# Issuing the up matrices of three of four experts from ScalarE's queue

## The chip, the cores and the metric

The kernel runs on one core of one Trainium2 chip. The metric is the device time of one execution in microseconds; of several runs the median is given. A "unit" below is one half of an expert's weight matrix, a transfer of 2048 KB (128 partitions of 4096 float32 numbers).

## What is computed

One inference step of one decoder layer: a combined projection, differential attention and a short convolution, an output projection, and a mixture of experts. The change touches the last of these alone. For 264 tokens (256 prompt rows and 8 sample rows) it is

```
y = (silu(xblk @ w_gate[e]) * (xblk @ w_up[e])) @ w_down[e]   # for each of 32 experts, float32
x = x + sum over the token's two experts of weight * y
```

`w_gate[e]` and `w_up[e]` are 2048 x 512, `w_down[e]` is 512 x 2048, each 4 MB. All 32 experts are read once, 192 units in all.

## The kernel before

**The ring.** All weights pass through `ring`, a buffer in SBUF of SLOTS = 8 slots, each of one unit. Units take the slots in turn: unit n goes to slot n % 8. A front part (projections, caches, output projection) uses the first units; the experts' units follow. Expert e has six (UPE = 6), numbered i = 0 to 5 in the order in which TensorE uses them: gate halves 0 and 1, up halves 2 and 3, down halves 4 and 5. Experts go in groups of EG = 4 (j = 0 to 3), eight groups; a loop over the groups g runs on each engine.

**Who issues.** Before the change SyncE (SP) issues every unit, in that same order (`stream_unit`, L499 to L503). Ahead of each it waits until the unit that had the slot eight units earlier has been used (`expert_used`, L505 to L511): `unit_used` for a gate or up half 0, `g_done` for gate half 1, `u_done` for up half 1, `down_half` and `down_done` for the down halves. So the up halves of expert e+1 take the slots of the gate halves of expert e. When a unit has landed, the semaphore `slot_full` of its slot is raised, and TensorE waits for it in `weights` (L897 to L905). One unit is an exception: the first up half of the second expert of all (m == SLOTS, L528 to L535) is issued in two parts of 1024 KB, the first as soon as TensorE has made four of the eight products of the slot's old unit (`half_used`).

**TensorE's order for one expert** (L969 to L1008): gate half 0 (`unit_products`, L912), mixing of the previous expert's output into bank 4 to 7 and 2 (L958, L952), gate half 1, the second mix, up half 0, the turning of the gate weights (L965), the gathering of the rows of the next expert (L852), up half 1, the fold of gate and up (L922, L923), the turning of the next expert's rows (L860) and of the hidden row (L929), and the two down halves (L937). VectorE adds the mixed output to `xa` (L1648, L1652), multiplies (L1665) and copies (L1663, L1667).

**ScalarE's order for one expert** (L1238 to L1257): it waits for `g_done`, copies the gate product from PSUM to `g_sb` (L1241), and then, each after a wait of its own, copies the turned gate weights (`copy_gate`, L1247), the gathered rows (L1218), makes the silu (L1253) and copies the down product to `ye` (L1257). In the first expert of a group `copy_gate` comes after the silu. Ahead of the loop it makes the exponentials and four moves of sample rows (L1226 to L1230). Far ahead of that, near the kernel's start, it makes copies (L1041, L1048, L1049, L1051, L1055) and behind them in the program issues small loads (L1060) and a store of 2112 KB (L1074) on its own DMA queue, which the profile calls q10; SyncE's queue is q1.

**The end.** After the last expert TensorE mixes once more, VectorE adds, SyncE stores `y_prompt` (L564) and ScalarE `y_sample` (L1261).

Of the kernel before, what the change touches and what calls it, by code (L numbers as in the profile page):

```python
# [21 lines left out]
KT = D // P  # L22
# [23 lines left out]
SLOTS = 8  # L46
UNIT = 4096
# [4 lines left out]
EG = 4  # L52
# [4 lines left out]
UPE = 6  # L57
# [11 lines left out]
NFRONT = len(FRONT)  # L69
# [73 lines left out]
def build(nc, ins, outs):  # L143
    ctx = ExitStack()
    with ctx:
        def sb(name, shape, dt=F32):
            return ctx.enter_context(nc.sbuf_tensor(name, shape, dt))

        def sem(name):
            return ctx.enter_context(nc.semaphore(name))  # L150

        ring = sb("ring", [P, SLOTS, UNIT])
# [13 lines left out]
        def const(name):  # L166
            a, b = CONST_AT[name]
            return consts[:, a:b]
# [37 lines left out]
        o = [0]  # L206
# [93 lines left out]
        slot_full = [sem(f"slot_full{i}") for i in range(SLOTS)]  # L300
# [103 lines left out]
        hidden_T = sem("hidden_T")  # L404
        act_ready = sem("act_ready")
        unit_used = sem("unit_used")
        half_used = sem("half_used")
        half_in = sem("half_in")
        down_half = sem("down_half")
        down_done = sem("down_done")  # L410
        ye_copied = sem("ye_copied")
# [8 lines left out]
        def slot_of(n):  # L420
            return n % SLOTS
# [12 lines left out]
        def used_wait(eng, n):  # L434

            kind, u = FRONT[n]
            if kind == "KP":
                eng.wait_ge(page_sum, PPU * (u + 1))
            elif kind == "QB":
                eng.wait_ge(page_mul, 8 * (u + 1))  # L440
            elif kind == "VP":
                eng.wait_ge(s_pv, u + 1)
            else:
                eng.wait_ge(tile_done, TILE_AT[(kind, TPU * u + TPU - 1)] + 1)
# [5 lines left out]
        def _(sp):  # L450
# [5 lines left out]
            for n, (kind, u) in enumerate(FRONT):  # L456
                s = slot_of(n)
# [22 lines left out]
                elif kind in ("KP", "VP"):  # L480
# [3 lines left out]
                    for i in range(PPU):  # L484
                        j = u * PPU + i
# [10 lines left out]
            wu = ins["w_up"].rearrange("l (g j) (p k) f -> (l g) p j (k f)", j=EG, k=KT)  # L496
            wd = ins["w_down"].rearrange("l (g j) (p k) d -> (l g) p j (k d)", j=EG, k=FC)

            def stream_unit(g, j, i, s):  # L499

                half = i % 2
                src = (wg, wu, wd)[i // 2][bass.ds(g, 1), :, j, half * UNIT:(half + 1) * UNIT].rearrange("o p n -> p (o n)")
                sp.dma_start(ring[:, s, :], src).then_inc(slot_full[s], 16)  # L503

            def expert_used(m, it):  # L505

                j, i = divmod(m, UPE)
                if i in (0, 2):
                    sp.wait_ge(unit_used, it * (2 * EG) + (2 * j + i // 2 + 1))
                else:  # L510
                    sp.wait_ge({1: g_done, 3: u_done, 4: down_half, 5: down_done}[i], it * EG + (j + 1))  # L511

            def group(g, it):

                for j in range(EG):
                    for i in range(UPE):
                        m = j * UPE + i
                        s = slot_of(NFRONT + m)

                        expert_used(m - SLOTS, it)  # L520
                        stream_unit(g, j, i, s)

            for m in range(UPG):
                s = slot_of(NFRONT + m)
                j, i = divmod(m, UPE)
                if m < SLOTS:
                    used_wait(sp, NFRONT + m - SLOTS)
                elif m == SLOTS:  # L528

                    sp.wait_ge(half_used, 1)  # L530
                    src = wu[0, :, j, 0:UNIT]
                    sp.dma_start(ring[:, s, 0:UNIT // 2], src[:, 0:UNIT // 2]).then_inc(half_in, 16)
                    expert_used(0, 0)
                    sp.dma_start(ring[:, s, UNIT // 2:], src[:, UNIT // 2:]).then_inc(slot_full[s], 16)
                    continue  # L535
                else:
                    expert_used(m - SLOTS, 0)
                stream_unit(0, j, i, s)
            with sp.Fori(1, NG) as g:
                group(g, g)  # L540
# [3 lines left out]
            with sp.If(npass > 1):  # L544
                with sp.Fori(1, npass) as r:
                    with sp.Fori(0, NG) as g:
                        group(g, r * NG + g)
# [24 lines left out]
        def _(pe):  # L572
# [5 lines left out]
            for t in range(2):  # L578
                pe.wait_ge(x_in[t], 16)
                for g in range(4):  # L580
                    if t == 1 and g == 3:
                        pe.wait_ge(xT_dve, 1)
                    for kk in range(4):
                        k = 4 * g + kk
                        m = pe.transpose(bank[(X0_BANKS, X1_BANKS)[t][g]][:, kk * P:(kk + 1) * P], xa[:, t, k * P:(k + 1) * P], ident)
# [227 lines left out]
            for t in range(TT):  # L813
                n = P if t < 2 else NB
                m = pe.matmul(bank[3][0:n, P + t:P + t + 1], sacc[:, t * P:t * P + n], const("ones")[:, 0:1], start=True, stop=True)
# [4 lines left out]
            for t in range(TT):  # L820
                n = P if t < 2 else NB
                m = pe.transpose(bank[5][0:n, t * RE:(t + 1) * RE], logitsT[:, t * P:t * P + n], ident[64:64 + RE, 64:64 + RE])
# [62 lines left out]
            for half in range(2):  # L885
                pe.wait_ge(xrow_copied, half + 1)
                for m_ in (2 * half, 2 * half + 1):
                    m = pe.transpose(bank[(5, 7)[half]][:, m_ * P:(m_ + 1) * P], xrow[:, m_ * P:(m_ + 1) * P], ident)
# [4 lines left out]
            with pe.Fori(0, npass) as r:  # L893
                with pe.Fori(0, NG) as g:
                    it = r * NG + g

                    def weights(j, i):  # L897

                        m = j * UPE + i
                        s = slot_of(NFRONT + m)  # L900
                        before = sum(slot_of(NFRONT + x) == s for x in range(m + 1))
                        pe.wait_ge(slot_full[s], it * (16 * UPG // SLOTS) + (front_total[s] + 16 * before))
                        if m == SLOTS:
                            pe.wait_ge(half_in, 16)
                        return ring[:, s, :]  # L905

                    def unit_products(j, b, i):

                        w = weights(j, 2 * b + i).rearrange("p (k f) -> p k f", f=F)
                        for x in range(8):  # L910
                            k, c = 8 * i + x, x % 4
                            m = pe.matmul(bank[b][c * C:(c + 1) * C, :], xeT[j % 2][:, k, :], w[:, x, :],  # L912
                                          start=i == 0 and x < 4, stop=i == 1 and x >= 4, skip_group_check=True)
                            if (j, b, i, x) == (0, 0, 0, 3):
                                m.then_inc(half_used, 1)
                        m.then_inc((unit_used, (g_done, u_done)[b])[i], 1)

                    def fold(e):
# [13 lines left out]
                    def down(j, i):  # L932

                        w = weights(j, 4 + i).rearrange("p (c d) -> p c d", c=FC // 2)
                        for c in range(FC // 2):
                            for n in range(4):
                                m = pe.matmul(bank[2][n * C:(n + 1) * C, :], actT[:, i * FC // 2 + c, :], w[:, c, n * 512:(n + 1) * 512],  # L937
                                              start=i == 0 and c == 0, stop=i == 1 and c == FC // 2 - 1, skip_group_check=True)
                        m.then_inc((down_half, down_done)[i], 1)
# [77 lines left out]
        def _(act):  # L1017
# [123 lines left out]
            for n in range(NIN):  # L1141
# [4 lines left out]
                elif (n - BCX) % 3 == 0:  # L1146
                    i = (n - BCX) // 3
# [11 lines left out]
                if stage == 0 and 0 <= h < H:  # L1159

                    act.wait_ge(biased, h + 1)
                    for x in range(4):
                        a, b = ((0, 256), (256, 512), (512, 640), (640, 768))[x]
# [40 lines left out]
            for at in Y_ORDER:  # L1204
                if at is None:
                    continue
                t, g = at
                act.wait_ge(y_T, n_turned + 1)
                n = P if t < 2 else NB
# [4 lines left out]
            def copy_rows(e):  # L1214

                act.wait_ge(gathered, e + 1)
                act.wait_ge(xe_T, e)
                A(xrow, bank[4][:, :], ACT.Copy).then_inc(xrow_copied, 1)  # L1218
# [12 lines left out]
                  h2s.rearrange("p (c m q) -> p q m c", c=4, m=4)[:, 32 * n:32 * n + 32], ACT.Copy).then_inc(xs_moved, 1)  # L1231

            act.wait_ge(routed, 1)
            npass = act.value_load(npass_sb[0:1, 0:1], min_val=1, max_val=MAXPASS)
            with act.Fori(0, npass) as r:
                with act.Fori(0, NG) as g:
                    it = r * NG + g
                    for j in range(EG):  # L1238
                        e = it * EG + j
                        act.wait_ge(g_done, e + 1)  # L1240
                        A(g_sb, bank[0][:, :], ACT.Copy).then_inc(g_copied, 1)  # L1241

                        def copy_gate():

                            act.wait_ge(gate_T, e + 1)
                            act.wait_ge(mixed, it * NSTEPS + (NSTEPS + (STEP_AT[(1, j - 1)] + 1 if j else 0)))
                            A(gateT, bank[5][:, 0:TT * P].rearrange("p (t s) -> p t s", t=TT), ACT.Copy).then_inc(gateT_copied, 1)  # L1247

                        if j >= 1:
                            copy_gate()  # L1250
                        copy_rows(e + 2)
                        act.wait_ge(folded, e + 1)
                        A(hidden, bank[3][0:C, :], ACT.Silu).then_inc(silu_done, 1)  # L1253
                        if j == 0:
                            copy_gate()
                        act.wait_ge(down_done, e + 1)
                        A(ye, bank[2][:, :], ACT.Copy).then_inc(ye_copied, 1)  # L1257
# [536 lines left out]
```

## Time and profile before

| | before |
|---|---|
| median of 3 runs | 1460.32 us (1460.26 to 1462.41) |
| the profiled execution | 1459.15 us, span 1457.0 us |
| TensorE busy | 1224.4 us, 84% of the span |
| ScalarE busy | 221.8 us, 15% |
| DMA, queue q1 (SyncE) | 495.32 MB |
| DMA, queue q10 (ScalarE) | 7.07 MB |

The span is the part of the profiled execution between its first and last instruction; 2.15 us of the execution lie outside it. The median is 1.17 us above the profiled execution. The rows in the section of rows are copied from the profile and its trace; times in them are counted from the start of the span.

### The profile page before, as it was taken

The numbers are of one execution on the slowest core, as the hardware profiler recorded it, in microseconds if no ns is written. First come the engines' busy times: TensorE is split into PE (matmuls) and PEld (weight loads), VectorE is DVE, ScalarE is ACT, GpSimd is POOL, SyncE is SP. The second block draws the span as 40 slices with busy tenths as digits, with TensorE's granted clock in tenths as the row PEclk, the third lists the DMA queues.
The fourth block names the chain that finished last, engine by engine and source line by source line (L and its number), as shares of the span: only waits on it lengthen the run. The fifth ranks groups of instructions, "written<-read, shape, count | busy, mean of one in ns | idle before, by whom it ended". The sixth has DMA issues, their size and how long they took to land.

```text
span 1457.0 us, 20094 instructions
## 1 busy us (share of the span) xinstructions
PE 1224.4 (84%) x8331; PEld 640.5 (44%) x8331; DVE 491.5 (34%) x950; ACT 221.8 (15%) x443; POOL 53.6 (4%) x40
## 2 busy tenths in 40 slices
PE   9999999999999988877777777777777777877776
PEld 8888888888788852221221222122222222212221
DVE  4332138684111152433332332332233333242223
ACT  3111232312000041110010011011101011001100
POOL 0000003241000020000000000000000000000000
PEclk9999999999999999999999999999999999899989
DMA  9975334659395449999999999999999999999997
GB/s 342 349 225 172 135 130 139 223 192 326 116 356 232 151 158 428 428 428 428 428 428 429 428 429 428 428 430 428 429 427 430 426 430 428 429 428 429 428 428 299
DMA packets 107675, 503.52 MB, mean 346 GB/s; under 512 B 6286, under 2 KB 76614, under 8 KB 82166
## 3 DMA queue, kind: packets, MB, share of 16 engines
q1 hardware_dynamic: 100338, 495.32, 84.3%
q10 hardware_dynamic: 6996, 7.07, 1.4%
q0 software_dynamic: 304, 0.61, 0.2%
q8 instruction: 26, 0.43, 0.1%
q14 instruction: 11, 0.09, 0.0%
HBM read 496.42 MB, written 6.59 MB: 345 GB/s over the span
## 4 chain that ended last, share of the span: by engine, by line
PE 50%; DMA 44%; DVE 4%; issue 1%; ACT 1%; ACTq 0%; DVEq 0%; SPq 0%
PE bank L638 31%; DMA ring<-in_w_up 22%; DMA ring<-in_w_gate 16%; PE bank L912 6%; DMA ring<-in_w_down 5%; PE bank L937 3%; PE bank L852 2%; DVE xa L1652 1%; PE bank L958 1%; PE bank L922 1%; PE bank L965 1%; DVE bc L1663 1%; PE bank L929 0%; PE bank L649 0%; PE bank L729 0%
## 5 line engine op out<-in xcount | busy, mean ns | idle before, releaser
L912 PE MATMUL bank<-ring,bc 128*32 128x512 f32 x2048 | 259.2, 628 | 128.0 <-DMA ring<-in_w_gate 61.3
L638 PE MATMUL bank<-bc,ring 128*128 128x264 f32 x1536 | 350.8, 387 | 1.3 <-DVE bc L1301 1.3
L638 PEld LDWEIGHTS bank<-bc,ring 128*128 128x128 f32 x1536 | 288.6, 190 | 51.1 <-issue 2.3
L1652 DVE TENSOR_TENSOR xa<-xa,bank 128x512 f32<-128x512 f32 x256 | 158.7, 682 | 303.5 <-PE bank L958 303.5
L912 PEld LDWEIGHTS bank<-ring,bc 128*32 128x32 f32 x2048 | 58.7, 112 | 314.2 <-issue 185.5
L937 PE MATMUL bank<-ring,cat 128*32 128x512 f32 x1024 | 151.0, 734 | 25.2 <-DVE cat L1667 17.3
L638 PE MATMUL bank<-cat,ring 128*128 128x264 f32 x512 | 116.0, 388 | 0.0
L638 PEld LDWEIGHTS bank<-cat,ring 128*128 128x128 f32 x512 | 96.7, 190 | 18.9 <-issue 2.9
L1663 DVE COPY bc<-bank 128x512 f32<-128x512 f32 x32 | 22.1, 692 | 222.1 <-PE bank L912 222.1
L937 PEld LDWEIGHTS bank<-ring,cat 128*32 128x32 f32 x1024 | 35.0, 127 | 115.6 <-issue 83.0
L958 PE MATMUL bank<-bc 32*128 32x512 f32 x512 | 73.9, 647 | 6.4 <-ACT bc L1257 6.4
L852 PE MATMUL bank<-cat,bc 128*32 128x512 f32 x512 | 62.2, 603 | 0.0
L1323 DVE RECIPROCAL xa<-xa 128x264 f32<-128x264 f32 x16 | 28.8, 1803 | 85.3 <-ACT xa L1091 85.3
L1241 ACT ACTIVATE bc<-bank 128x512 f32<-128x512 f32 x32 | 19.1, 597 | 251.2 <-PE bank L912 251.2
L922 PE MATMUL bank<-bc,consts 128*32 128x512 f32 x64 | 32.6, 590 | 29.0 <-DVE bc L1663 29.0
L1257 ACT ACTIVATE bc<-bank 128x512 f32<-128x512 f32 x32 | 19.1, 597 | 230.1 <-PE bank L937 230.1
L860 PE MATMUL bank<-consts,bc 128*128 128x128 f32 x128 | 26.4, 298 | 28.1 <-DVE bc L1665 21.9
L958 PEld LDWEIGHTS bank<-bc 32*128 32x128 f32 x512 | 20.4, 187 | 65.2 <-issue 45.1
L1695 POOL TENSOR_TENSOR ring<-ring 128x1024 f32<-128x1024 f32 x16 | 37.6, 2375 | 283.9 <-DVE xa L1372 283.9
L1665 DVE TENSOR_TENSOR bc<-bc,bank 32x512 f32<-32x512 f32 x32 | 21.8, 680 | 59.3 <-ACT bc L1253 59.3
L1503 DVE TENSOR_TENSOR bc<-bc,bank 128x264 f32<-128x264 f32 x16 | 6.9, 429 | 99.4 <-PE bank L638 99.4
L860 PEld LDWEIGHTS bank<-consts,bc 128*128 128x128 f32 x128 | 14.1, 140 | 56.0 <-issue 28.4
(272 smaller groups left out, 858.3 us busy)
## 6 DMA issues: line engine op xcount, KB each, us to landing
ring<-in_w_gate SPq DMA_DIRECT2D x64, 2048.0 KB, 34.8
ring<-in_w_down SPq DMA_DIRECT2D x64, 2048.0 KB, 36.8
ring<-in_w_up SPq DMA_DIRECT2D x63, 2048.0 KB, 36.8
ring<-in_w_in SPq DMA_DIRECT2D x23, 2048.0 KB, 13.8
ring<-in_w_out SPq DMA_DIRECT2D x8, 2048.0 KB, 16.5
ring<-in_cache_k SPq DMA_DIRECT2D x16, 512.0 KB, 5.2
ring<-in_cache_v SPq DMA_DIRECT2D x16, 512.0 KB, 8.1
ring<-qrows_scratch SPq DMA_DIRECT2D x2, 2048.0 KB, 7.0
```

The costliest lines, as they stand in the source:

```text
L638: m = pe.matmul(bank[n % 3][:, 0:T], w[:, k, (i % TPU) * P:(i % TPU + 1) * P], src[:, k, :], start=n_k == 0, stop=n_k == KT - 1)
L852: m = pe.matmul(bank[4][c * C:(c + 1) * C, :], lhs, rhs, start=t == 0, stop=t == TT - 1, skip_group_check=True)
L860: m = pe.transpose(bank[5][:, m_ * P:(m_ + 1) * P], xrow[:, m_ * P:(m_ + 1) * P], ident)
L912: m = pe.matmul(bank[b][c * C:(c + 1) * C, :], xeT[j % 2][:, k, :], w[:, x, :], start=i == 0 and x < 4, stop=i == 1 and x >= 4, skip_group ...
L922: pe.matmul(bank[3][0:C, :], const("fold"), g_sb, start=True, stop=True, skip_group_check=True)
L937: m = pe.matmul(bank[2][n * C:(n + 1) * C, :], actT[:, i * FC // 2 + c, :], w[:, c, n * 512:(n + 1) * 512], start=i == 0 and c == 0, stop= ...
L958: m = pe.matmul(bank[to[n]][:, :], gateT[rows_, t, :], ye[rows_, :], start=True, stop=True)
L1323: st.do(V.reciprocal(r, r))
L1652: V.tensor_tensor(xa[:, t, cols], xa[:, t, cols], bank[to[n]][:, :], ALU.add).then_inc(mix_added, 1)
L1663: V.tensor_copy(u_sb, bank[1][:, :]).then_inc(u_copied, 1)
L1665: V.tensor_tensor(hidden, hidden, bank[3][C:2 * C, :], ALU.mult).then_inc(hidden_ready, 1)
L1695: G.tensor_tensor(kp, kp, ring[:, sq_, (b % 4) * ATT:(b % 4 + 1) * ATT], ALU.mult).then_inc(page_mul, 1)
```

## The change

SyncE no longer issues the up halves of the experts j = 1, 2 and 3 of each group. ScalarE issues both, in expert j - 1, directly behind its copy of the gate product, with no wait of its own: `g_done` of expert j - 1 tells that both gate halves have been used, whose slots they take. The up halves of j = 0 stay with SyncE. The exception at m == SLOTS falls away with its two semaphores. Of the experts' 192 units 48 are issued by ScalarE.

```
@@ SyncE, group()
                         s = slot_of(NFRONT + m)
+                        if j >= 1 and i in (2, 3):
+                            continue
                         expert_used(m - SLOTS, it)
                         stream_unit(g, j, i, s)
@@ SyncE, the first group
                     used_wait(sp, NFRONT + m - SLOTS)
-                elif m == SLOTS:
-                    sp.wait_ge(half_used, 1)
-                    src = wu[0, :, j, 0:UNIT]
-                    sp.dma_start(ring[:, s, 0:UNIT // 2], src[:, 0:UNIT // 2]).then_inc(half_in, 16)
-                    expert_used(0, 0)
-                    sp.dma_start(ring[:, s, UNIT // 2:], src[:, UNIT // 2:]).then_inc(slot_full[s], 16)
+                elif i in (2, 3):
                     continue
@@ TensorE, weights() and unit_products()
-                        if m == SLOTS:
-                            pe.wait_ge(half_in, 16)
...
-                            if (j, b, i, x) == (0, 0, 0, 3):
-                                m.then_inc(half_used, 1)
@@ ScalarE
+            wu_act = ins["w_up"].rearrange("l (g j) (p k) f -> (l g) p j (k f)", j=EG, k=KT)
...
                         act.wait_ge(g_done, e + 1)
                         A(g_sb, bank[0][:, :], ACT.Copy).then_inc(g_copied, 1)
+                        if j < EG - 1:
+                            for half in range(2):
+                                s = slot_of(NFRONT + (j + 1) * UPE + 2 + half)
+                                src = wu_act[bass.ds(g, 1), :, j + 1, half * UNIT:(half + 1) * UNIT].rearrange("o p n -> p (o n)")
+                                act.dma_start(ring[:, s, :], src).then_inc(slot_full[s], 16)
```

ScalarE at the loop's second expert, before. `bank0` holds the gate product, `bank5` the turned gate weights; a wait in brackets is the semaphore that the instruction waits for:

```order
L1241 ACTIVATE bc<-bank0 128x512 [waits g_done]
L1246 REGISTER_ALU [waits gate_T]
L1247 ACTIVATE bc<-bank5 128x384 [waits mixed]
L1216 REGISTER_ALU
L1218 ACTIVATE bc<-bank4 128x512 [waits xe_T,gathered]
```

The same place in the changed kernel, whose line numbers are lower by nine:

```order
L1232 ACTIVATE bc<-bank0 128x512
L1238 ISA
L1238 DMA ring<-in_w_up 128x4096
L1238 ISA
L1238 DMA ring<-in_w_up 128x4096
L1243 REGISTER_ALU
L1244 ACTIVATE bc<-bank5 128x384
```

Two issues, each with one register instruction, now stand between the copy of the gate product and the copy of the turned gate weights.

SyncE at the entry of the experts, before, from the last units that wait for the front part on:

```order
L503 DMA ring<-in_w_gate 128x4096 [waits tile_done] x2
L532 DMA ring<-in_w_up 128x2048 [waits half_used]
L534 DMA ring<-in_w_up 128x2048 [waits unit_used]
L503 DMA ring<-in_w_up 128x4096 [waits g_done]
L503 DMA ring<-in_w_down 128x4096 [waits unit_used]
L503 DMA ring<-in_w_down 128x4096 [waits u_done]
L503 DMA ring<-in_w_gate 128x4096 [waits down_half]
L503 DMA ring<-in_w_gate 128x4096 [waits down_done]
```

And in the changed kernel:

```order
L501 DMA ring<-in_w_gate 128x4096 [waits tile_done] x2
L501 DMA ring<-in_w_down 128x4096 [waits unit_used]
L501 DMA ring<-in_w_down 128x4096 [waits u_done]
L501 DMA ring<-in_w_gate 128x4096 [waits down_half]
L501 DMA ring<-in_w_gate 128x4096 [waits down_done]
```

The three rows on the up matrix are gone from SyncE; the waits of the others are the same.

## Rows read from the trace of the kernel before

**Rows 1.** The page: DMA busy tenths and GB/s in 40 slices of the span.

```profile
DMA  9975334659395449999999999999999999999997
GB/s 342 349 225 172 135 130 139 223 192 326 116 356 232 151 158 428 428 428 428 428 428 429 428 429 428 428 430 428 429 427 430 426 430 428 429 428 429 428 428 299
```

**Rows 2.** Busy time of each engine in one stretch, clock, DMA share, GB/s.

```profile
546.00:1440.00 894.00, 678.03 (x5628) 197.19 (x5620) 278.49 (x528) 109.32 (x173) 0.00 (x0) 0.94 1.01 428
```

**Rows 3.** Timeline of TensorE, one expert: start us, us, engine line, work.

```profile
924.03 1.92 PE L912 MATMUL bank<-ring,bc 128*32 128x512 f32 x16 [0.82 <-DMA ring<-in_w_gate]
928.92 1.92 PE L912 MATMUL bank<-ring,bc 128*32 128x512 f32 x16 [1.90 <-DMA ring<-in_w_up]
...
948.60 3.58 PE L912 MATMUL bank<-ring,bc 128*32 128x512 f32 x16 [2.31 <-DMA ring<-in_w_gate]
```

**Rows 4.** The page: DMA issues, KB each, us from issue to landing.

```profile
ring<-in_w_up SPq DMA_DIRECT2D x63, 2048.0 KB, 36.8
```

**Rows 5.** Timeline of SyncE's queue as the experts begin.

```profile
538.40 0.33 SPq L532 DMA_DIRECT2D ring<-in_w_up  x1
...
540.97 0.33 SPq L503 DMA_DIRECT2D ring<-in_w_up  x1
542.69 4.89 SPq L503 DMA_DIRECT2D ring<-in_w_down  x2
```

**Rows 6.** Timeline of ScalarE as the experts begin.

```profile
536.36 4.53 ACT L1230 ACTIVATE xa<-bc 8x512 f32<-8x512 f32 x4
540.90 1.28 ACT L1241 ACT_TABLE_LOAD   x1
542.20 0.60 ACT L1241 ACTIVATE bc<-bank 128x512 f32<-128x512 f32 x1
```

**Rows 7.** Timeline of ScalarE and its queue near the kernel's start.

```profile
12.77 0.27 ACT L1051 ACTIVATE ring<-bank,consts 128x8 f32<-128x8 f32 x1
12.79 0.35 ACTq L1060 DMA_DIRECT2D ring<-in_lam_q  x1
...
14.37 0.30 ACT L1055 ACTIVATE small<-bank 128x128 f32<-128x128 f32 x1
```

**Rows 8.** DMA from 16 to 18.5 us, issues: KB each, us to landing.

```profile
ring<-in_w_in SPq DMA_DIRECT2D x2, 2048.0 KB, 25.2
small<-in_g_sub ACTq DMA_DIRECT2D x1, 0.5 KB, 6.0
```

**Rows 9.** DMA from 18.5 to 30.7 us: queues, and the store of L1074.

```profile
q1 hardware_dynamic: 2303, 2.34, 58.8%
q10 hardware_dynamic: 884, 2.20, 46.8%
...
xT_scratch<-cat ACTq DMA_DIRECT2D x1, 2112.0 KB, 12.1
```

**Rows 10.** Timeline of TensorE, the second expert: every unit had landed.

```profile
561.34 1.92 PE L912 MATMUL bank<-ring,bc 128*32 128x512 f32 x16
...
564.26 1.92 PE L912 MATMUL bank<-ring,bc 128*32 128x512 f32 x16
...
570.44 1.92 PE L912 MATMUL bank<-ring,bc 128*32 128x512 f32 x16
...
577.29 3.64 PE L937 MATMUL bank<-ring,cat 128*32 128x512 f32 x32 [0.66 <-DVE cat L1667]
```

**Rows 11.** Timeline of TensorE, the last expert and the last mixes.

```profile
1423.28 1.93 PE L912 MATMUL bank<-ring,bc 128*32 128x512 f32 x16 [0.81 <-DMA ring<-in_w_gate]
...
1428.17 1.92 PE L912 MATMUL bank<-ring,bc 128*32 128x512 f32 x16 [1.90 <-DMA ring<-in_w_up]
...
1440.14 5.29 PE L937 MATMUL bank<-ring,cat 128*32 128x512 f32 x32 [0.56 <-DVE cat L1667]
1446.23 1.14 PE L958 MATMUL bank<-bc 32*128 32x512 f32 x8 [0.80 <-ACT bc L1257]
```

**Rows 12.** Waits from 560 to 1440 us: total us, times, longest.

```profile
ACT bc L1241 <- PE bank L912: 251.2, 31, 10.0
ACT bc L1247 <- PE bank L965: 116.3, 31, 6.7
```

More of the change, by code:

```diff
@@ L406, in build @@
         unit_used = sem("unit_used")
-        half_used = sem("half_used")
-        half_in = sem("half_in")
         down_half = sem("down_half")
```

## The prediction

> **What bounds the kernel now.** I read the page's 40 slices first. From the sixteenth slice to the last but one the DMA engines are busy in nine tenths or more and move 426 to 430 GB/s [rows 1], and for the 894 us from 546 to 1440 they are at a share of 1.01 with 428 GB/s, while TensorE is busy for 678 us of these [rows 2]. So the experts' stage is bound by the transfers. The pace shows on TensorE: the second gate half of an expert starts at 924.03 and that of the last expert, 17 experts later, at 1423.28 [rows 3, 11], 29.37 us an expert, 4.895 us a unit. TensorE waits for a unit and uses it in 1.92 us: gate half 1 at 924.03 and up half 0 at 928.92 are one unit apart [rows 3]. A unit lands 36.8 us after its issue [rows 4]: seven units of work, 34.3 us, and 2.5 us besides. The queue is always deep. In such a stage the order or the issuer of the transfers can change the time in three ways only: when the stream starts, whether it ever runs dry or slow, and how much work TensorE still has when the stream ends.
>
> **The start of the stream, +2.65 us.** When the experts begin, the ring is full and the DMA engines idle. The stream starts with the split up half at 538.40, the next up half follows when both gate halves are used, at 540.97, the first down half at 542.69 [rows 5]. The change removes the early start. ScalarE waits for the same event as the issue at 540.97. Its engine is then busy with moves (until 540.90), loads a table and starts the copy only at 542.20 [rows 6], but its issues need not wait for that: near the start a transfer of L1060 goes out at 12.79, although L1055, which stands ahead of it in the program, runs only at 14.37 [rows 7]. So I put ScalarE's first issue at 541.05, which is 540.97 and a little for a register instruction, and the stream starts 541.05 - 538.40 = 2.65 us later. If the issues did wait for the engine they would go out after 542.8, and the down half at 542.69 would lead: 4.3 us is the upper bound. The lower is 2.6, from 538.40 to 540.97. From there on the same amount of data must come at the same pace, so every later landing of the whole stream shifts by this.
>
> **ScalarE's time, 0.** Each issue is 0.35 us on its queue [rows 7]; two and their registers make some 0.8 us behind the copy of the gate product. The next thing that ScalarE does waits for TensorE's turning of the gate weights, 116.3 us in 31 waits, 3.8 us each [rows 12]; that covers it. Without the cover it would be 24 x 0.8 = 19 us of delay to a copy that TensorE needs, but still not of the stream. ScalarE's own wait for `g_done` ends 251.2 us of idle time in 31 waits [rows 12], so it is always there in time.
>
> **SyncE, 0.** It is moved past nothing: its down and gate issues keep their waits, and none of these comes later because an up issue is gone. The up half 0 of an expert is now issued at `g_done` rather than when gate half 0 is used, one unit later; the queue still holds over five units then.
>
> **The order of landing.** The trace has two hints on how the two queues share the engines. Two loads of SyncE issued from 16 to 18.5 us took 25.2 us to land, while a small one of ScalarE took 6.0 [rows 8]; and the store of 2112 KB that ScalarE issued at 18.55 landed in 12.1 us, while q1 moved 2.34 MB and q10 2.20 MB [rows 9]. So ScalarE's queue does not stand behind what SyncE queued earlier, and two full queues share about equally.
>
> Now walk one expert with time 0 at the landing of gate half 1 of expert e. Its up halves have already landed (issued an expert ago). Queued on q1 are down 0, down 1 of e and gate 0, gate 1 of e+1, 19.6 us of work. TensorE starts some 2.5 us after the engines are done (the 2.5 above), needs 2 us for the half, and ScalarE's two units, issued at 5, begin to move at about 6 (an estimate, within 1 us of no account). Until 26 they take half the rate. In that time q1 moves down 1 and gate 0 (done at 13 and 23), and gate 1 of e+1 is done at 29.4. This is again six units, so the period is unchanged: at every moment four or more units are outstanding, and the stream never runs dry. What changes is the order: the up halves land ahead of the gate halves of the same expert, and **gate half 1 is the third from last of an expert's units to land, no longer the fifth**: only down 0 and down 1 come behind it.
>
> **The end of the stream, +7.2 us.** Inside the stage TensorE's slack hides the new order (19.6 us of work behind gate half 1, next gate half 0 at 24.5). The last expert has no successor to hide it. Before, its gate half 1 starts at 1423.28 and down ends at 1440.14 + 5.29 = 1445.43 [rows 11]: 22.15 us. After, the two up halves have gone ahead of gate half 1, so it starts 2 x 4.895 = 9.79 us later, and all that follows on TensorE still has to be done: gate half 1, mix, up half 0, turning and gathering, up half 1, fold, silu, turning, two down halves. The second expert shows what this chain takes when every unit lies in the ring: from 561.34 to 577.29 + 3.64 = 580.93, 19.59 us [rows 10]. So 9.79 + 19.59 - 22.15 = 7.23 us. The last mixes, adds and stores follow as before. An upper bound is another 3.4 us: after idle time the same 16 products took 3.58 us at 948.60 instead of 1.92 [rows 3], and a longer idle time ahead of the gate half may bring two such slow halves into the last chain. The lower bound is 0, if all units still landed in the order of issue.
>
> **Sum.** 2.65 + 0 + 0 + 7.23 = 9.9 us. The profiled execution would take 1459.15 + 9.9 = 1469.0 us, and the median, 1.17 us above, **1470.2 us**. Bounds of the terms: 2.6 to 4.3, and 0 to 10.6.
>
> **Rivals.** A: the queues are served in the order of issue, or ScalarE's has almost no precedence. Then only the start is lost: +2.65, 1463.0 us. Against it stand [rows 8, 9], for it that no row shows both queues full of units like these. If ScalarE's share were a third, up half 1 would land last but one and the tail would be about +4: 1467. B, the other side: two queues together move data faster than one. Each per cent of pace is worth 9.0 us over the 900 us of the stream, so it decides from 1.1% on, 428 to 433 GB/s; at 1.5% the time is 1470.2 - 13.5 = 1456.7. Against it: q1 alone already has the engines at a share of 1.01 [rows 2] and its best slice is 430 [rows 1]. The Trainium skill (DMA: Bandwidth & Descriptors, Rules for kernel authors) says that spreading DMAs over issuers doesn't help the bandwidth and saves issue time only. By that rule B gains nothing and the sum stays at 1470.2 instead of 1456.7. No run here has yet shown two queues of large loads together. C: two streams from different matrices are served worse than one, at 0.5 to 1% less pace, +4.5 to 9: 1475 to 1479. The stretch with both queues active [rows 9] averages 4.56 MB in 12.2 us, 374 GB/s, but it mixes loads with a store and says little. D: the change does not do what it says, since ScalarE reaches its issue late: excluded, by its waits [rows 12].
>
> **How the numbers follow.** The forecast has 0.60 and covers 1467 to 1474; A 0.13, a third of it at 1466 or so; B 0.10, of which 0.07 below 1457.4; C 0.17. The range of 8 in 10 takes in A's 1463.0 and most of C: 1462 to 1479. A measurement of this kernel tells about 0.2%, 2.9 us, from no change: faster is below 1457.4, slower above 1463.2. A's pure form lies at that line. Faster 0.07, same 0.11, slower 0.82.
>
> **What would show it.** In the profile after: 48 units on ScalarE's queue, landing in about 22 us, SyncE's gate units in about 30; first ScalarE issue near 541.05; 428 GB/s in the stretch from 550 to 1440; up half 0 following gate half 1 within 3 us without a wait in experts j = 1 to 3; and from the last expert's gate half 1, at about 1435.7, to the end of its down product at 1455.3, 19.6 us. An issue at 542.8 makes the start term 4.3; ScalarE's units landing in 35 us make A right; a pace other than 428 GB/s makes B or C right and moves the sum by 9 us a per cent.

## The result

The changed kernel takes 1471.42 us (median of 4 runs, 1471.30 to 1471.74) against 1460.29 us; the ratio is 1.0072 with a 95% interval of 1.0061 to 1.0084, some 9 to 12 us slower. Run again beside the experiments it came out at 1.0076 (1.0063 to 1.0090). The forecast was 1470.2 us. One run of the kernel before, among those beside e1 to e4, took 3095.6 us and is left out everywhere. The profiled execution took 1471.30 us with a span of 1469.1 us, 12.1 us more than the span before.

From the page of the changed kernel, its 40 slices and its two hardware queues (packets, MB, share of the 16 engines):

```profile
DMA  9974344658494439999999999999999999999995
GB/s 342 348 235 155 132 132 163 230 190 287 149 369 194 157 144 428 428 428 428 429 428 428 428 429 428 428 429 428 428 429 429 428 429 428 428 428 429 429 428 201
q1 hardware_dynamic: 93282, 394.66, 67.5%
q10 hardware_dynamic: 13908, 107.74, 17.6%
```

The stage of the experts is still one unbroken row of nines at 428 GB/s, as in [rows 1]. A hundred MB have moved from q1 to q10 and the pace is the same. The stretch of [rows 2] shows it in one line (TensorE, weight load, VectorE, ScalarE, GpSimd busy, then clock, DMA share, GB/s):

```profile
546.00:1440.00 894.00, 681.28 (x5548) 196.68 (x5548) 274.56 (x521) 108.16 (x170) 0.00 (x0) 0.92 1.01 428
```

The landing times on the page (KB each, median us from issue to landing) tell that the queues do not stand behind one another:

```profile
ring<-in_w_gate SPq DMA_DIRECT2D x64, 2048.0 KB, 34.1
ring<-in_w_down SPq DMA_DIRECT2D x64, 2048.0 KB, 29.3
ring<-in_w_up ACTq DMA_DIRECT2D x48, 2048.0 KB, 17.2
```

An up half used to take 36.8 us [rows 4]. Issued by ScalarE it takes 17.2. In a stretch in which both queues are full, 920 to 927 us, they split the bytes nearly in half:

```profile
q1 hardware_dynamic: 100, 1.56, 52.2%
q10 hardware_dynamic: 103, 1.43, 47.9%
```

So the time must have gone at the two ends of the stream. **The start**, ScalarE and its queue in the timeline of the changed kernel:

```profile
539.96 1.28 ACT L1232 ACT_TABLE_LOAD   x1
541.80 0.60 ACT L1232 ACTIVATE bc<-bank 128x512 f32<-128x512 f32 x1 [0.55 <-PE bank L904]
541.95 0.96 ACTq L1238 DMA_DIRECT2D ring<-in_w_up  x2
```

The first issue stands at 541.95, where [rows 5] have 538.40: 3.55 us later. The issue goes out while the copy of 541.80 is still running, so it does not wait for the end of that copy. **The end**, TensorE in the timeline of the changed kernel, last expert and last mixes:

```profile
1436.64 1.92 PE L904 MATMUL bank<-ring,bc 128*32 128x512 f32 x16 [2.65 <-DMA ring<-in_w_gate]
...
1439.56 1.92 PE L904 MATMUL bank<-ring,bc 128*32 128x512 f32 x16
...
1445.73 1.92 PE L904 MATMUL bank<-ring,bc 128*32 128x512 f32 x16
...
1452.48 5.20 PE L927 MATMUL bank<-ring,cat 128*32 128x512 f32 x32 [0.56 <-DVE cat L1664]
1458.48 1.14 PE L948 MATMUL bank<-bc 32*128 32x512 f32 x8 [0.80 <-ACT bc L1254]
```

In [rows 11] up half 0 began with a wait of 1.90 us for its transfer; here it follows with no DMA wait, since it landed long before. The last wait for a transfer is that of gate half 1. It starts at 1436.64 instead of 1423.28, 13.36 us later, and this is 3.55 us of start and 9.81 us for the two up halves that overtook it. From it to the end of the down product are now 1452.48 + 5.20 - 1436.64 = 21.04 us instead of 22.15. In sum 3.55 + 9.81 - 1.11 = 12.25 us on TensorE, and the span grew by 12.1; what follows the last down product took 11.42 us instead of 11.57.

### The profile page after: what moved, and what is told of

It is laid out like the page before. It is cut to its first block, busy times and chain, and to the rows that moved or that the text cites. A ratio compares the mean times of both kernels' runs of the same rounds, so it can differ in the third digit from the quotient of the medians.

```text
span 1469.1 us, 20120 instructions
## 1 busy us (share of the span) xinstructions
PE 1236.2 (84%) x8331; PEld 640.9 (44%) x8331; DVE 491.3 (33%) x950; ACT 221.8 (15%) x443; POOL 53.5 (4%) x40
## 4 chain that ended last, share of the span: by engine, by line
PE 55%; DMA 37%; DVE 6%; issue 1%; ACT 1%; SPq 0%; ACTq 0%; DVEq 0%
DMA ring<-in_w_gate 36%; PE bank L632 31%; PE bank L904 7%; PE bank L927 4%; PE bank L846 3%; DVE xa L1649 3%; PE bank L948 2%; PE bank L912 1%; PE bank L955 1%; DVE bc L1660 1%; DVE bc L1662 1%; PE bank L919 1%; ACT bc L1250 1%; PE bank L942 1%; DMA xa<-in_x_prompt 1%
## 5 line engine op out<-in xcount | busy, mean ns | idle before, releaser
L904 PE MATMUL bank<-ring,bc 128*32 128x512 f32 x2048 | 268.5, 651 | 112.8 <-DMA ring<-in_w_gate 98.2
L927 PE MATMUL bank<-ring,cat 128*32 128x512 f32 x1024 | 149.3, 732 | 24.4 <-DVE cat L1664 17.2
L948 PE MATMUL bank<-bc 32*128 32x512 f32 x512 | 78.3, 683 | 6.4 <-ACT bc L1254 6.4
L955 PE MATMUL bank<-consts,bc 128*32 128x128 f32 x768 | 30.8, 277 | 18.0 <-DVE xa L1649 18.0
L955 PEld LDWEIGHTS bank<-consts,bc 128*32 128x32 f32 x768 | 21.2, 109 | 43.4 <-DVE xa L1649 39.8
## 6 DMA issues: line engine op xcount, KB each, us to landing
ring<-in_w_gate SPq DMA_DIRECT2D x64, 2048.0 KB, 34.1
ring<-in_w_up ACTq DMA_DIRECT2D x48, 2048.0 KB, 17.2
```

Source lines behind the costliest of these rows:

```text
L948: m = pe.matmul(bank[to[n]][:, :], gateT[rows_, t, :], ye[rows_, :], start=True, stop=True)
L955: m = pe.matmul(bank[5][c * C:(c + 1) * C, t * P:(t + 1) * P], gate[:, t, j * C:(j + 1) * C], ident, start=True, stop=True, skip_group_che ...
```

## The experiments

Theory T puts the time at the two ends. Theory R is its rival: two queues disturb each other all along, and each unit on the second one costs a little (11.1 us over 48 units are 0.23 us each). All differences below are ratios to the kernel before, run on the same chip, times 1460.4 us, with 95% intervals. In the diffs `...` leaves lines out. These kernels are built on the changed kernel (e1, e5) or on the kernel before (the others).

### e1: ScalarE issues for j = 1 only

```
-                        if j >= 1 and i in (2, 3):
+                        if j in (1,) and i in (2, 3):
...
-                        if j < EG - 1:
+                        if j + 1 in (1,):
```

> ScalarE issues only the up halves of the experts j = 1 (16 units); the split of the first up half falls away as in the changed kernel; the last expert's up halves are SyncE's again. Theory T (the time is lost at the two ends: a later start of the stream, and more of TensorE's work behind the last gate half): only the start is left, +2.6 to +3.6 us, the last expert from its gate half 1 to the end of its down product takes some 22 us as before. Theory R (the two queues disturb each other all along the stage, in proportion to the units on ScalarE's queue, 11.1 us / 48 = 0.23 us each): +3.7 us. This run alone doesn't tell them apart by the time, but by where the last expert's gate half 1 begins: T has it 2.6 to 3.6 us later, and the stream at 428 GB/s.

Measured: +2.9 us (1.6 to 4.2). The last expert waits for its transfers as before, and takes 1446.57 + 5.41 - 1429.71 = 22.3 us from gate half 1 on (TensorE, timeline of e1):

```profile
1429.71 1.92 PE L904 MATMUL bank<-ring,bc 128*32 128x512 f32 x16 [0.27 <-DMA ring<-in_w_gate]
1434.60 1.92 PE L904 MATMUL bank<-ring,bc 128*32 128x512 f32 x16 [1.90 <-DMA ring<-in_w_up]
```

Both theories forecast this size; the next runs part them. What T said of the last gate half 1 did not come out. In this profiled execution, the slowest of the ten of e1 (1465.58 us), the last gate half 1 begins 1429.71 - 1423.28 = 6.43 us later than before, where T had 2.6 to 3.6. Nearly all of it is in the start: the first issue stands 6.18 us later than before (ScalarE's queue in e1), and the granted clock was 0.50 from 536 to 542 us.

```profile
544.58 0.96 ACTq L1238 DMA_DIRECT2D ring<-in_w_up  x2
```

### e2: ScalarE issues for j = 2 only

```
+                        if j + 1 in (2,):
+                            for half in (0, 1):
+                                ...
+                                act.dma_start(ring[:, s, :], src).then_inc(slot_full[s], 16)
```

with SyncE leaving these units out, and the split of the first up half kept.

> ScalarE issues only the up halves of the experts j = 2 (16 units); the split of the first up half is kept, and the last expert's up halves are SyncE's. T: neither end is touched, 0 us (within 0.5). R: 16 units at 0.23 us, +3.7 us.

Measured: +2.3 us (0.9 to 3.8). Neither forecast fits: T said 0 and R 3.7. The pace from 546 to 1430 us is 428 GB/s as everywhere. But the end of the timeline shows something that T had overlooked (TensorE in e2, expert 30 from its gate half 1 on, then expert 31):

```profile
1404.73 1.92 PE L915 MATMUL bank<-ring,bc 128*32 128x512 f32 x16 [0.81 <-DMA ring<-in_w_gate]
...
1420.58 3.64 PE L940 MATMUL bank<-ring,cat 128*32 128x512 f32 x32 [0.56 <-DVE cat L1676]
1424.04 1.91 PE L915 MATMUL bank<-ring,bc 128*32 128x512 f32 x16
...
1427.93 1.92 PE L915 MATMUL bank<-ring,bc 128*32 128x512 f32 x16
...
1443.95 6.18 PE L940 MATMUL bank<-ring,cat 128*32 128x512 f32 x32 [0.56 <-DVE cat L1676]
```

No product of the last expert waits for a transfer. Expert 30 got its gate half 1 late, its chain of 19.5 us ended at 1424.2, and the last expert had to be done from there without a pause. It is the same mechanism one expert earlier: the lateness is passed on, because the last expert's own units are on time and TensorE isn't. I call this T'; e9 tests it. The last down product ran at the lower clock as well (6.18 us, where it took 5.29 before), so a part of this profile's loss is the clock's.

### e3: ScalarE issues for j = 3 only

The same edit with `(3,)`.

> ScalarE issues only the up halves of the experts j = 3 (16 units), the last expert's among them; the split of the first up half is kept. T: the end alone, +7.2 us, up to +8.7 if the last down product again runs at the lower clock; the last expert from gate half 1 to the end of the down product takes 19.6 to 21 us and begins 9.8 us later. R: +3.7 us.

Measured: +9.2 us (6.6 to 11.7). The end term alone carries most of the change's cost, with a third of its units on ScalarE's queue. R's 3.7 is outside. From the last gate half 1 to the end of the down product (TensorE in e3) it is 1455.92 - 1436.44 = 19.48 us:

```profile
1430.59 3.64 PE L915 MATMUL bank<-ring,bc 128*32 128x512 f32 x16 [1.34 <-DMA ring<-in_w_gate]
...
1436.44 1.92 PE L915 MATMUL bank<-ring,bc 128*32 128x512 f32 x16
...
1452.28 3.64 PE L940 MATMUL bank<-ring,cat 128*32 128x512 f32 x32 [0.56 <-DVE cat L1676]
```

Gate half 1 begins 13.16 us later than before. Of this 9.79 are the two units and 1.58 the first issue (539.98 against 538.40). The remaining 1.79 are about what gate half 0 ahead of it lost by running in 3.64 us, at the lower clock, instead of 1.92; gate half 1 itself shows no wait for its transfer.

### e4: the same order of landing, on SyncE's queue alone

```
-                    for i in range(UPE):
+                    for i in (range(UPE) if j < EG - 1 else (2, 3, 0, 1, 4, 5)):
```

> Nothing on ScalarE's queue. SyncE issues all units, but for the experts j = 3 of all groups except the first it issues the two up halves ahead of the two gate halves, so that they land in the order which the changed kernel gives them. T: the order of landing is what costs at the end, so this costs the same as ScalarE's issue for j = 3: +7.2 to +8.7 us. R, or any theory that needs the second queue: 0 us.

Measured: +7.9 us (5.5 to 10.4), against an expected 7.2 to 8.7. Nothing of the experts is on q10 in this kernel. The last expert (TensorE in e4):

```profile
1430.40 3.64 PE L912 MATMUL bank<-ring,bc 128*32 128x512 f32 x16 [12.14 <-DMA ring<-in_w_gate]
...
1436.10 1.92 PE L912 MATMUL bank<-ring,bc 128*32 128x512 f32 x16
...
1451.95 3.64 PE L937 MATMUL bank<-ring,cat 128*32 128x512 f32 x32 [0.56 <-DVE cat L1667]
```

Again 1455.59 - 1436.10 = 19.49 us, and again gate half 0 ran in 3.64 us and gate half 1 did not wait for its transfer. The second queue isn't needed for the loss. What costs is that the last expert's gate halves land behind its up halves.

### e5: the changed kernel with j = 3 given back to SyncE

The edit of e1 with `(1, 2)`.

> The changed kernel with the up halves of the experts j = 3 given back to SyncE: ScalarE issues 32 units, none of them of the last expert. T: the start alone, +2.6 to +3.6 us, as with 16 units. R: 32 units at 0.23 us, +7.4 us.

Measured: +6.9 us (4.5 to 9.2), twice what T said, and near to R's 7.4. The time alone would speak for R. The trace does not: the pace is 428 GB/s with 32 units on q10, and the last expert looks like that of e2 (TensorE in e5):

```profile
1423.45 6.14 PE L927 MATMUL bank<-ring,cat 128*32 128x512 f32 x32 [0.56 <-DVE cat L1664]
...
1433.30 1.92 PE L904 MATMUL bank<-ring,bc 128*32 128x512 f32 x16
...
1449.14 5.25 PE L927 MATMUL bank<-ring,cat 128*32 128x512 f32 x32 [0.55 <-DVE cat L1664]
```

The down product of expert 30 takes 6.14 us, at the lower clock, and ends at 1429.59; the last expert follows without a wait. Start term (e1, 2.9) and passed-on lateness (e2, 2.3) make 5.2 us, inside the interval. From its first issue, at 541.98, to the end of its last down product e5 takes 912.41 us; e2, with half the units on q10, takes 912.52 (from 537.61). So in these profiles the sixteen additional units cost nothing between the two points.

### e6: half of the overtaking

The edit of e3 for up half 0 only; up half 1 stays with SyncE.

> ScalarE issues only up half 0 of the experts j = 3; up half 1 is SyncE's; the split of the first up half is kept. T: one unit overtakes instead of two, so the last gate half 1 begins 4.9 us later than before, not 9.8, and the chain of 19.6 us follows: 4.9 + 19.6 - 22.15 = +2.3 us, up to +3.8 with a down product at the lower clock. R: 16 or fewer units at 0.23 us, and half the bytes of the run with j = 3 alone, so half of its cost.

Measured: +3.1 us (1.5 to 4.7). One unit that overtakes costs a third of what two cost (e3, 9.2); a half, 4.6, lies at the very edge of the interval, and e3's own interval is wide, so the two times alone do not decide. A third is T's arithmetic (2.3 of 7.2): 22.15 - 19.5 = 2.65 us of the delay cost nothing. Not all of this is time in which TensorE waited for later units: in the 22.15 us the last down product ran at the lower clock (5.29 us), in the 19.5 at the full one (3.64).

### e7 and e10: the start of the stream without the second queue

e7 takes the split away; e10 holds the first up half back to the event on which ScalarE issues:

```
-                elif m == SLOTS:
-                    sp.wait_ge(half_used, 1)
-                    ...
+                elif m == SLOTS:
+                    expert_used(1, 0)
```

> The kernel before without the split of the first up half: SyncE issues it whole when gate half 0 is used. T: the stream starts at what was 539.25 instead of 538.40, +0.85 us. A theory in which the start of the stream costs nothing: 0.

> Nothing on ScalarE's queue. The kernel before without the split, and with the first up half held back until both gate halves have been used (the event on which the changed kernel's ScalarE issues), so both up halves go out together at the time that was 540.97. T: the start term alone, +2.6 us at the full clock, up to +3.7 where TensorE's first products run at the lower clock; no change in the last expert. A theory in which only ScalarE's issue or the second queue costs: 0.

Measured: e7 +0.1 us (-1.2 to 1.5), which cannot tell 0.85 from 0. e10 +1.8 us (0.4 to 3.1), so T's 2.6 is inside and 0 outside. The timeline of e10, SyncE and TensorE:

```profile
540.74 0.80 SPq L503 DMA_DIRECT2D ring<-in_w_up  x2
```

```profile
537.05 5.36 PE L904 MATMUL bank<-ring,bc 128*32 128x512 f32 x48 [1.95 <-DVE bc L1589]
...
1425.57 1.92 PE L904 MATMUL bank<-ring,bc 128*32 128x512 f32 x16 [0.83 <-DMA ring<-in_w_gate]
```

The first expert begins at 537.05 there and at 537.27 before. From that to the last gate half 1 are 888.52 us in e10 and 1423.28 - 537.27 = 886.01 before: 2.51 us more, with nothing on ScalarE's queue. The late start is a cost by itself and is not ScalarE's.

### e9: half of the overtaking, for j = 2

The edit of e2 for up half 0 only.

> ScalarE issues only up half 0 of the experts j = 2; all else as before. With both up halves of j = 2 on ScalarE's queue the time rose by 2.3 us, which T did not foresee; T': the overtaking moves the last gate half 1 of expert 30 by 9.8 us, its chain of 19.6 us then ends 4.8 us behind the landing of the last expert's gate half 0, and the last expert, without idle time, can't make that up. With one unit overtaking, the chain ends just as that gate half lands: 0 to +0.7 us (the latter if the down product of expert 30 runs at the lower clock), and the last expert waits for its transfers again. R' (each unit on the second queue costs 2.3 us / 16): +1.2 us and no such waits in the last expert.

Measured: -0.9 us (-2.2 to 0.3). R' with +1.2 is outside, and T' with 0 inside its interval. The last expert waits for its transfers again (TensorE in e9):

```profile
1416.57 5.12 PE L940 MATMUL bank<-ring,cat 128*32 128x512 f32 x32 [0.56 <-DVE cat L1676]
1421.52 1.89 PE L915 MATMUL bank<-ring,bc 128*32 128x512 f32 x16
...
1429.33 1.92 PE L915 MATMUL bank<-ring,bc 128*32 128x512 f32 x16 [0.93 <-DMA ring<-in_w_up]
...
1441.29 1.92 PE L940 MATMUL bank<-ring,cat 128*32 128x512 f32 x16 [0.56 <-DVE cat L1676]
1443.97 1.92 PE L940 MATMUL bank<-ring,cat 128*32 128x512 f32 x16 [0.76 <-DMA ring<-in_w_down]
```

The down product of expert 30 is slow here too (5.12 us), yet up half 0 of the last expert has a wait of 0.93 us: the lateness has been made good by then. Eight units on the second queue that delay no last chain cost nothing that can be measured. The last two rows show the last down product at the full clock: its second half waits 0.76 us for its transfer, so there the landing sets the end.

### e8: both ends finer than before

```
+                    for q in range(2):
+                        sp.wait_ge(half_used, q + 1)
+                        sp.dma_start(... quarter q ...).then_inc(half_in, 16)
...
+                if (j, i) == (EG - 1, UPE - 1):
+                    sp.dma_start(ring[:, s, 0:UNIT // 2], src[:, 0:UNIT // 2]).then_inc(last_half, 16)
+                    sp.dma_start(ring[:, s, UNIT // 2:], src[:, UNIT // 2:]).then_inc(slot_full[s], 16)
```

TensorE's waits and signals for the parts are left out here.

> The kernel before with both ends finer: the first up half goes out in a quarter after two products, a quarter after four and a half; and the last down half of each group comes in two parts of 1024 KB, of which TensorE uses the first while the second still lands. T: the stream starts 0.45 us sooner, and the last product ends 0.9 us sooner: -1.0 to -1.4 us in all. If the ends don't set the time: 0.

Measured: +1.0 us (-0.3 to 2.3); the gain of 1.0 to 1.4 us did not come. At the end TensorE ran the down products at the lower level, as this row of e8 shows (32 products in 5.34 us and no wait for a transfer; at the full clock 3.64):

```profile
1443.81 5.34 PE L950 MATMUL bank<-ring,cat 128*32 128x512 f32 x32 [0.56 <-DVE cat L1680]
```

With that, the product and not the landing sets the end, and the earlier half unit is of no use. It was the same in the kernel before (5.29 us in one piece, [rows 11]), so the 0.9 us that T wanted to save were not there in its profile. At the start this execution had a granted clock of 0.50 from 536 to 543 us, so its first issue came at 540.17 in spite of the quarter. Besides, from the first issue to the last gate half 1 e8 takes 1426.95 - 540.17 = 886.78 us, and the kernel before 1423.28 - 538.40 = 884.88; no run shows why. Whether the finer start gains anything at the full clock stays open.

### The changed kernel again

> The changed kernel once more, beside the two others on one chip: T: start term and end term together, 3.7 + 8.6 less what the clock at the entry gives or takes, +10 to +12 us.

Measured: +11.1 us (9.2 to 13.1). Nothing tried beats the kernel before clear of noise.

### All profiles on one scale

The profiled executions differ in when the stream starts, by the change and by the clock. Counted from the first issue of the experts' stream to the end of the last down product, that drops out:

| kernel | units on q10 | first issue | end of last down product | between, us |
|---|---|---|---|---|
| before | 0 | 538.40 | 1445.43 | 907.03 |
| e10, late start | 0 | 540.74 | 1447.78 | 907.04 |
| e7, no split | 0 | 541.79 | 1448.93 | 907.14 |
| e1, j = 1 | 16 | 544.58 | 1451.98 | 907.40 |
| e9, j = 2, one half | 8 | 538.38 | 1445.89 | 907.51 |
| e8, finer | 0 | 540.17 | 1449.15 | 908.98 |
| e6, j = 3, one half | 8 | 539.22 | 1449.83 | 910.61 |
| e5, j = 1 and 2 | 32 | 541.98 | 1454.39 | 912.41 |
| e2, j = 2 | 16 | 537.61 | 1450.13 | 912.52 |
| changed kernel | 48 | 541.95 | 1457.68 | 915.73 |
| e3, j = 3 | 16 | 539.98 | 1455.92 | 915.94 |
| e4, order alone | 0 | 539.23 | 1455.59 | 916.36 |
| changed kernel again | 48 | 543.46 | 1461.09 | 917.63 |

These are single executions, and the clock puts one or two microseconds into each. The list follows the order of landing in the last two experts and not the number of units on q10: kernels with 0, 16 and 48 units stand together at some 916 us, others with 0, 8 and 16 at 907. R, at 0.23 us a unit, would put 3.7 us between 0 and 16 units and 11 between 0 and 48. The passed-on lateness is 5.5 us here (e2), more than the 2.3 of its time. Of the 5.5, 0.79 go to the early first issue of e2's profile, and 1.16 to the kernel before, whose profiled execution is that much below the median of its runs beside e2. The 3.5 that are left lie inside e2's interval of 0.9 to 3.8.

## Why the prediction was right

**The bound.** It was read from the right rows. In every kernel here, with 0 to 48 units on ScalarE's queue, the stretch from 546 to 1430 us moved 428 GB/s. Rivals B and C, a faster or a slower stream, fall with that; what e9 measured bounds a cost of the second queue by itself at 0.3 us for 8 units, and e1's row of the table is 0.4 us above that of the kernel before, with 16 units. The rule of the Trainium skill that was set against B (DMA: Bandwidth & Descriptors, Rules for kernel authors) holds here: issuing from two engines gave no bandwidth, 428 GB/s with either.

**The order of landing.** Rival A, service in the order of issue, falls with the landing time of 17.2 us and the equal split from 920 to 927 us. The rows from which equal shares were taken [rows 8, 9] were of other transfers, but held. My landing times for the units were rough: 22 us for an up half and 30 for a gate half, where the medians are 17.2 and 34.1; neither entered the sum, which needs only that both up halves land ahead of gate half 1.

**The start, forecast +2.65 us.** The issue goes out 0.15 us behind the beginning of the copy and ahead of its end; in all 24 pairs of issues of this profile it is 0.13 to 0.41 us. It was never seen ahead of a copy that had still to begin, as in [rows 7]: when the event came, the table load at 539.96 was already over, so whether the issue would have passed it was not put to the test. By itself the term is 2.51 us (e10, from TensorE's first product on). In the profiled execution it was 3.55, and this is made of more than the change. Its first expert began at 536.40, 0.87 us sooner than before, and its 48 first products took 7.05 us instead of 5.36, as the granted clock was 0.72 from 536 to 542 us:

```profile
536.40 7.05 PE L904 MATMUL bank<-ring,bc 128*32 128x512 f32 x48 [1.96 <-DVE bc L1596]
```

So the event that ScalarE waits for, the end of both gate halves, is one that a low clock delays more than the first four products. Its issue stands 5.55 us behind the first product, where in e10 it is 3.69; before, the first issue stood 1.13 us behind it. That gives (3.69 - 1.13) + (5.55 - 3.69) - 0.87 = 3.55 us: 2.56 for the change, 1.86 for the clock, less the 0.87. The prediction had no clock in this term, which it mis-sized by 0.9 us in this profile; the change's own 2.56 lies close to the forecast 2.65.

**The end, forecast +7.23 us.** Its parts: 9.79 for the two units (measured 9.81), the chain of 19.59 us from [rows 10] (19.48 in e3, 19.49 in e4) and 22.15 before. In the changed kernel's profile the chain took 21.04 us, 1.45 more, as the last down product ran for 5.20 us instead of 3.64; that is the clock, for which the prediction had an upper bound of 3.4 us (twice 1.66, which is 3.3) and took 0. The term measured 9.81 + 21.04 - 22.15 = 8.70 us, 1.5 more than forecast. The sum compared unlike things here. Its 22.15 us of before hold a last down product of 5.29 us, its 19.59 us of after one of 3.64 us. At the full clock the chain of before would end sooner too, but not by all of the 1.65: in e9 it ends 1445.89 - 1429.33 = 16.56 us behind the start of up half 0, against 17.26 before. With the full clock on both sides the term is then about 7.9 us, an estimate from these rows. In e3 and e4 the last down product is fast, and the clock takes its share at gate half 0 instead. The runs show the mechanism from both sides: with ScalarE (e3) and without (e4), whole and in half (e6).

**The step that was wrong without harm.** The prediction said that inside the stage TensorE's slack hides the new order. It does so only while the following experts' units are late as well. In the changed kernel they are: gate half 1 of the last expert still waited 2.65 us. Where only j = 2 overtakes (e2, e5) the last expert's units come on time, there is no slack, and expert 30's lateness reaches the end. Even in the changed kernel the last expert's gate half 0 started without a wait, at 1430.00, right behind a down product of 5.34 us. The walk had 4.9 us of waiting ahead of that half. All that was left is the 2.65 us ahead of gate half 1.

**The other side.** Costs of ScalarE's time and of SyncE at 0 held. ScalarE's two issues take 0.84 us, and behind them it still waits 4.02 us for the turned gate weights (ScalarE of the changed kernel, the third expert):

```profile
585.87 0.84 ACTq L1238 DMA_DIRECT2D ring<-in_w_up  x2
590.36 0.49 ACT L1244 ACTIVATE bc<-bank 128x384 f32<-128x384 f32 x1 [4.02 <-PE bank L955]
```

The sum by the profiles is 3.55 + 8.70 = 12.25 against 9.9 forecast. The medians moved by 11.1, one less: the profiled execution of the kernel before is 1.14 us below its median and that of the changed kernel at its own. So the forecast of the median came nearer than its terms did. Both terms were short by the clock, 0.9 and 1.5 us, and 1.0 of these 2.4 us does not show in the medians, because of which execution of the kernel before was profiled. That part is luck.

## What to carry to other kernels

In a stage bound by transfers, ask of any change of issuer or order only this: when does the stream start, does it ever stop, and how much work still hangs on the last units to land. A transfer on a second queue overtakes what the first queue holds, so put there nothing whose early landing makes the longest chain of the last stage wait; the operand at the head of the longest chain should land first and the one with the least behind it last. When a change costs nothing in the middle, look at the last two rounds of the loop by themselves before calling it free.

## What was not expected of the hardware

TensorE's granted clock at the entry of the experts differs from one execution to the next. From 536 to 542 us it was 1.00 in the profiles of the kernel before, of e4, e9 and e10, 0.72 in those of the changed kernel, of e2, e5 and e6, 0.50 in those of e1, e3, e7 and e8, and 0.51 in that of the changed kernel again; 1.00 is the level of 2.4 GHz, 0.50 that of 1.2, and 0.72 a change between them. The changed kernel and e9 in that stretch (busy times, then clock, DMA share, GB/s):

```profile
536.00:542.00 6.00, 5.60 (x39) 1.61 (x43) 4.63 (x7) 5.36 (x6) 6.00 (x7) 0.72 0.01 3
```

```profile
536.00:542.00 6.00, 4.75 (x45) 1.52 (x49) 4.49 (x8) 5.90 (x8) 5.95 (x6) 1.00 0.45 153
```

The same 48 products took 5.36, 7.05 and up to 8.20 us (e3). Ahead of them TensorE had been idle for 2 us at most in each, waiting for VectorE. Where the clock was at 0.50 it had fallen earlier, behind an idle time of the same length: the kernel before, then e3 (TensorE):

```profile
530.89 1.28 PE L879 MATMUL bank<-cat,bc 128*32 128x256 f32 x16 [1.56 <-DVE bc L1580]
```

```profile
530.10 1.93 PE L882 MATMUL bank<-cat,bc 128*32 128x256 f32 x16 [1.56 <-DVE bc L1589]
```

The stream's start hangs on these products. The same event, the end of both gate halves, released the first issue at 540.74 in e10, 541.95 in the changed kernel, 543.46 in it again and 544.58 in e1. So the start of the stream moves by up to 3.8 us from one execution to the next, and this fits the spread of the runs of the kernel before, 1457.8 to 1463.5 us. That it is the cause of that spread is argued and not shown.
